# Values of 64-feature heads as the stationary operand, in two column tiles

## The reference, cut to what matters

```
s = q @ k.T * scale + bias[distance]          # causal
p = exp(s - max(s));  den = sum(p)            # rows of p are queries
y = (p @ v) / den                             # v: keys x 64 features
mix = concat(y of 8 heads of 64, y of 4 heads of 128) @ w_out
```

## Time and profile before

| | us |
|---|---|
| median of 3 runs | 2202.65 (2201.94 to 4978.07) |
| the profiled execution, its own time | 2203.65 |
| its span, first to last instruction | 2201.7 |
| MOBA units 8 to 15 | about 1156 to 1213 in the span |
| dil units 16 to 23 | about 1696 to 1755 in the span |

### The profile page before, as it was taken

The page is one execution under the profiler, slowest core; times in us unless marked ns, Lnnn a source line. Parts: engine busy times, 40 slices in busy tenths (PEclk is TensorE's granted clock), DMA queues, the critical chain, the costliest instruction groups (busy, mean ns, idle before and its releaser), DMA issues.

```text
span 2201.7 us, 27538 instructions
## 1 busy us (share of the span) xinstructions
PE 2173.0 (99%) x10078; PEld 1790.0 (81%) x10078; DVE 844.8 (38%) x1310; ACT 845.1 (38%) x1193; POOL 1048.5 (48%) x883
## 2 busy tenths in 40 slices
PE   8999999999999999999999999999999999999998
PEld 6778778888888888888888888888887888888887
DVE  4244666632451111222366633331226645232212
ACT  4245665422242222222366433332324734333321
POOL 5431244655544444555454354445554534444553
PEclk9999999999999999999999999999999999999999
DMA  5222122332223222333221232222332212222232
GB/s 180 88 78 77 39 88 85 99 111 96 96 85 107 95 95 78 105 104 99 103 63 63 77 115 95 95 77 93 108 113 91 74 47 96 95 95 98 84 103 78
DMA packets 33992, 201.89 MB, mean 92 GB/s; under 512 B 3900, under 2 KB 6204, under 8 KB 15484
## 3 DMA queue, kind: packets, MB, share of 16 engines
q1 hardware_dynamic: 31532, 192.94, 25.7%
q0 software_dynamic: 2384, 7.92, 1.1%
HBM read 198.69 MB, written 2.15 MB: 91 GB/s over the span
## 4 chain that ended last, share of the span: by engine, by line
PE 94%; DVE 3%; issue 1%; POOL 1%; ACT 1%; DMA 0%; DVEq 0%; SPq 0%; POOLq 0%; PEldq 0%; ACTq 0%
PE bank L417 28%; PE bank L419 28%; PE bank L418 28%; PE bank L660 2%; PE bank L958 1%; PE bank L647 1%; PE bank L918 1%; PE bank L972 1%; DVE pool_a L2346 1%; DVE temp_b L2162 0%; PE bank L634 0%; PE bank L633 0%; PE bank L630 0%; PE bank L1018 0%; PE bank L1019 0%
## 5 line engine op out<-in xcount | busy, mean ns | idle before, releaser
L1145 POOL TENSOR_TENSOR w_low<-raw,w_high 128x512 fp32r<-128x512 f32 (+2 forms) x768 | 961.3, 1283 | 1042.5 <-ACT w_high L1309 1004.1
L417 PE MATMUL bank<-x_low,w_high 128*128 128x512 f32 x1728 | 680.6, 394 | 13.1 <-DVE x_low L2158 9.4
L419 PE MATMUL bank<-x_high,w_low 128*128 128x512 f32 x1728 | 673.3, 390 | 0.0
L418 PE MATMUL bank<-x_high,w_high 128*128 128x512 f32 x1728 | 673.0, 389 | 0.0
L1309 ACT ACTIVATE w_high<-raw 128x2048 fp32r<-128x2048 f32 (+1 forms) x183 | 327.5, 1789 | 538.3 <-PE bank L419 538.3
L417 PEld LDWEIGHTS bank<-x_low,w_high 128*128 128x128 f32 x1728 | 324.8, 188 | 85.0 <-POOL w_low L1228 9.4
L418 PEld LDWEIGHTS bank<-x_high,w_high 128*128 128x128 f32 x1728 | 324.9, 188 | 68.5 <-issue 2.2
L419 PEld LDWEIGHTS bank<-x_high,w_low 128*128 128x128 f32 x1728 | 324.6, 188 | 68.3
L417 PE MATMUL bank<-act_low,w_high 128*128 128x512 f32 (+1 forms) x550 | 209.4, 381 | 0.0
L418 PE MATMUL bank<-act_high,w_high 128*128 128x512 f32 (+1 forms) x550 | 209.3, 381 | 0.0
L419 PE MATMUL bank<-act_high,w_low 128*128 128x512 f32 (+1 forms) x550 | 209.3, 380 | 0.0
(11 more groups left out here) (292 smaller groups left out, 2700.4 us busy)
## 6 DMA issues: line engine op xcount, KB each, us to landing
raw<-wmain SPq DMA_DIRECT2D x144, 1024.0 KB, 4.9
raw<-wdown SPq DMA_DIRECT2D x48, 704.0 KB, 4.0
bias<-distance_table POOLq DMA_DIRECT2D x24, 256.0 KB, 3.5
raw<-wmain SPq DMA_DIRECT2D x4, 512.0 KB, 8.5
x_residual<-x SPq DMA_DIRECT2D x4, 512.0 KB, 7.4
out<-qk SPq DMA_DIRECT2D x8, 256.0 KB, 2.2
matrices<-mats SPq DMA_DIRECT2D x1, 512.0 KB, 11.2
r_blocks<-rg POOLq DMA_DIRECT2D x1, 512.0 KB, 6.6
```

Of the source, the lines that this page charges most:

```text
L417: pe.matmul(target, sh, ml, start=start and k == 0, stop=False)
L418: pe.matmul(target, sh, mh, start=False, stop=False)
L419: last = pe.matmul(target, sl, mh, start=False, stop=stop and k == n - 1)
L1145: pool.tensor_tensor(wl[:, c, part], raw[:, c, part], wh[:, c, part].bitcast(F32), ALU.subtract).then_inc(low_ready, 1)
```

## The change

For MOBA and dil pairs, nothing is multiplied with the values in the even unit. Its turned probabilities are kept in `yt` (which no longer holds these heads' results). In the odd unit, `values` takes both heads: for each key block two matmuls, one for each head, with the 64 values of the head as the stationary operand and 128 turned probabilities as the moving one. The even unit's head takes column tile 0 and writes partitions 0 to 63 of bank 6, the odd one's takes column tile 64 and writes partitions 64 to 127. The result has features on the partitions and needs no turn. The norm factors, which are one for each token, are spread by DVE over 64 columns for each head (`rd` to `gs`), turned by PE with four transposes into a spare bank (`factors`), copied to `gs` by DVE, and multiplied with bank 6 back into the spare bank (`pair_normalised`); from there ACT and DVE take the high and low parts as before. The MOBA pairs' factors are turned in fills of units 10, 12 and 14 and in `project_out`. Renaming a helper (`paired` to `two_inputs`) changes nothing.

```diff
+def result_at(g):
+    return g // 2 if g < MLA else MLA // 2 + g - MLA
+
+def paired(g):
+    return MOBA <= g < MLA
+
-             + [("eturn", 2), ("eturn", 3)] + [("eout", t) for t in range(6)]
+             + [("eturn", 2), ("eturn", 3), ("eout", 0), ("eturn", 4), ("eout", 1), ("eout", 2), ("eturn", 5), ("eout", 3)]
+             + [("eout", 4), ("eturn", 6), ("eout", 5), ("eturn", 7)]
...
+        def turned(g, b):
+            if paired(g) and g % 2 == 0:
+                return yt[:, b, 0:(b + 1) * P]
+            return pts[:, b % 2, 0:(b + 1) * P]
...
             def values(g, b):
                 kind, m, u = UNITS[g]
+                if paired(g) and u == 0:
+                    return
                 v = turn_at(g)
                 pe.wait_ge(sem("pt_odd" if b % 2 else "pt_even"), 2 * v + b // 2 + 1)
-                if b == 0 and v:
-                    pe.wait_ge(sem("y_read"), v)
...
+                if b == 0 and result_at(g):
+                    pe.wait_ge(sem("y_read"), result_at(g))
+                if paired(g):
+                    for k in range(b + 1):
+                        for j, turned in enumerate((yt, pts)):
+                            at = 64 * j
+                            last = pe.matmul(bank[6][at:at + 64, b * P:(b + 1) * P], vt[:, k, m * P + at:m * P + at + 64],
+                                             turned[:, b % (2 if j else NB), k * P:(k + 1) * P], start=k == 0, stop=k == b,
+                                             tile_position=(0, at))
+                    last.then_inc(sem("pv_done"), 1)
+                    return
...
+            def factors(target, n):
+                pe.wait_ge(sem("rd_ready"), n + 1)
+                for b in range(NB):
+                    last = pe.transpose(target[:, b * P:(b + 1) * P], gs[:, n // HEADS, b * P:(b + 1) * P], ident)
+                return last
...
             def token_turn(n):
-                target = spare(("oturn", n))
-                pe.wait_ge(sem("y_read"), turn_at(DIL + 2 * n + 2))
-                turn(target, n).then_inc(sem("spare_ready"), 1)
+                factors(spare(("oturn", n)), HEADS + n).then_inc(sem("spare_ready"), 1)
...
                 elif g < DIL:
                     at = 4 * (g - 9) + b - 3
+                    if g % 2 == 0 and b == 3:
+                        factors(spare(("eturn", g // 2 - 1)), g // 2 - 5).then_inc(sem("spare_ready"), 1)
                     if at < 24:
                         first_half("eout", at // 4, at % 4)
...
-                    pe.wait_ge(sem("y_read"), turn_at(units) - heads * (3 - h))
-                    turn(bank[TURN_BANK[h]], first + h).then_inc(sem("turned"), 1)
+                    if name == "oout":
+                        pe.wait_ge(sem("y_read"), result_at(units) - (3 - h))
+                        turn(bank[TURN_BANK[h]], first + h).then_inc(sem("turned"), 1)
+                    elif h == 3:
+                        factors(spare(("eturn", 7)), 3).then_inc(sem("spare_ready"), 1)
...
+                        if t == 0 and name == "eout":
+                            spare_free(pe, ("eturn", HEADS + k))
...
             def normalised(g):
                 kind, n, u = UNITS[g]
-                dve.wait_ge(sem("pv_done"), 4 * turn_at(g) + 4)
+                if paired(g):
+                    dve.wait_ge(sem("p_ready"), score_at(g, 3) + 1)
+                    step(dve.reciprocal(rd[:, u, :], rs[:, u, :]))
+                    if u:
...
+                        dve.tensor_copy(gs[:, int(g > DIL), :].rearrange("p (b u f) -> p b u f", b=NB, u=2),
+                                        rd.rearrange("p u b -> p b u").unsqueeze(3).to_broadcast([P, NB, 2, 64]))\
+                           .then_inc(sem("rd_ready"), 1)
+                    return
...
+            def pair_normalised(r, target):
+                spread = gs[:, r // HEADS - 1, :]
+                step(dve.tensor_copy(spread, target))
+                dve.wait_ge(sem("pv_done"), 4 * r + 4)
+                dve.tensor_tensor(target, bank[6][:, :], spread, ALU.mult).then_inc(sem("y_read"), 1)
...
                     if b == 2:
                         half_added("eout", g - 10)
+                    if g % 2 == 0 and b == 3:
+                        dve.wait_ge(sem("spare_ready"), SPARE["eturn", g // 2 - 1] + 1)
+                        pair_normalised(g // 2 - 1, spare_bank(("eturn", g // 2 - 1)))
+                    if g % 2 and b == 0 and g > 10:
+                        pair_turn(g // 2 - 5)
```

More of the change, by code:

```diff
@@ L512, in token_major, with two_inputs @@
                                 behind_first()
[L514 removed]
+            def two_inputs(name, chunks, x0, x1, ready, read0, read1, free_after, x0_ready=None, x1_ready=None,
                        norm=None, at=0, free=None):
@@ L827, in fill, with project_out @@
                         first_half("oout", n // 4, n % 4)
-            def project_out(name, ready, read, units, turned):
-                first, heads = YT[name, 1], 2 if name == "eout" else 1
+            def project_out(name, ready, read, units):
+                first = YT[name, 1]
                 pe.wait_ge(sem("s_read"), 4 * units)
@@ L1425, in copy_even @@
                 if n >= 2:
-                    act.wait_ge(sem("pv_done"), n - 1)
-                act.activation(pts[:, 0, 0:(b + 1) * P], bank[4][:, 0:(b + 1) * P], ACT.Copy)\
-                   .then_inc(sem("pt_even"), 1)
+                    act.wait_ge(sem("pv_done"), copy_after(g, b))
+                act.activation(turned(g, b), bank[4][:, 0:(b + 1) * P], ACT.Copy).then_inc(sem("pt_even"), 1)
             def spare_refill(use, c, n, second):
@@ L1550, in spare_out @@
                     head_turn(2 + b // 2)
+                elif MOBA < g < DIL and g % 2 == 0 and b == 3:
+                    pair_turn(g // 2 - 5)
                 elif (g, b) == (MLA, 0):
@@ L1563, in spare_out, with project_out @@
                         mla_copy(("uv", n), vt[:, n, S:2 * S])
-            def project_out(name, ready, read, v, gain, g0, turned):
-                for h in range(4):
-                    act.wait_ge(sem("turned"), turned + h + 1)
-                    turn_high(name, 1, h, bank[TURN_BANK[h]][:, :])
+            def project_out(name, ready, read, v, gain, g0):
+                if name == "eout":
+                    pair_turn(3)
+                else:
+                    for h in range(4):
+                        act.wait_ge(sem("turned"), h + 1)
+                        turn_high(name, 1, h, bank[TURN_BANK[h]][:, :])
                 refill(1, BASE[name] + 3)
@@ L1989, in copy_odd @@
                 if n >= 2:
-                    dve.wait_ge(sem("pv_done"), n - 1)
-                dve.tensor_copy(pts[:, 1, 0:(b + 1) * P], bank[5][:, 0:(b + 1) * P]).then_inc(sem("pt_odd"), 1)
+                    dve.wait_ge(sem("pv_done"), copy_after(g, b))
+                dve.tensor_copy(turned(g, b), bank[5][:, 0:(b + 1) * P]).then_inc(sem("pt_odd"), 1)
             def blocks(t, n=P):
@@ L2147, in project_out @@
             def project_out(name, ready, read, v, gain, g0, high):
-                for h in range(4):
-                    turn_low(name, 1, h, bank[TURN_BANK[h]][:, :], high + h + 1, sem("turn_read"))
+                if name == "eout":
+                    dve.wait_ge(sem("spare_ready"), SPARE["eturn", 7] + 1)
+                    pair_normalised(result_at(DIL) - 1, spare_bank(("eturn", 7)))
+                    pair_turn(3)
+                else:
+                    for h in range(4):
+                        turn_low(name, 1, h, bank[TURN_BANK[h]][:, :], high + h + 1, sem("turn_read"))
                 spare_free(dve, (name, 4), (name, 5))
```

45 lines of the change are left out of this document (31 added, 14 removed).

## The result

The changed kernel takes **2206.97 us** (median of 18 runs, 2204.36 to 2209.84), the kernel before 2202.77 beside it: ratio 1.0019, 95% interval 1.0013 to 1.0026. So it is 4.2 us slower, where 5.6 us faster was forecast. The profiled execution of after took 2209.16 us, near the top of its runs, that of before 2203.65; what is read from the two traces therefore adds up to 5.5 us. One run of the kernel before took 4978.07 us and stands outside the ratio.

What follows compares the result with a forecast made beforehand. PE, busy for 99% of the span, was taken as the bound. Values and switches -7.5, dil's turns -0.7, projection's end +1.1 and new waits +1.5 gave -5.6 us: a median of 2197 us, range 2190 to 2206.

Steps and rivals of the forecast that it cites:

- Values and switches: MOBA and dil pairs: side-by-side tiles plus three switches of 0.34 take 3.22 us instead of 4.16; 7.5 us gained in all.
- two rivals: Tiled value blocks: weight loads not hidden, about 2206 us (5%); tiles take turns, about 2214 us (7%).
- The projection's end: Projection behind MOBA: the last operand waits for DVE's copy and multiplication of the turned factors, +1.1 us (0.7 to 1.4).
- The new waits: Paired stretches: DVE's and ACT's added factor work is mostly hidden, +1.5 us, between -1 and +9.7.
- The sign that the prediction named: Forecast is wrong if PE's idle time before the values (L681) or transposes (L665) grows by more than 3 us.
- The clock: Rival: more idle time on PE in dil could bring four clock drops, +6.8 us, near 2204; 3%.
- the waits take it back: Rival: DVE and ACT fall behind at seven places, +9.7 instead of +1.5, about 2205 us; 15%.
- the 15% rival: DVE and ACT fall behind at seven places in the paired stretches, +9.7 instead of +1.5, about 2205 us; 15%.
- The new order of the spare banks: Paired stretches: spare banks come free about as far ahead of the next fill's need as before; cost nothing.
- +1.5 - 0.7: Paired stretches: +1.5 us of new waits for DVE and ACT, -0.7 as dil's turns stop waiting for the factors' product.
- the 9.7 less 0.7 of the rival: +9.7 us if DVE and ACT fall behind at seven places (15%), less 0.7 of dil's turns' waits that go.

Runs made afterwards that it cites:

- e5: Changed kernel with the values of step 0 taken in step 2, so two tiled blocks for a pair instead of three: 2205.95 us.
- e3: Changed kernel with ACT making both high parts of the next stack in step 0 of the unit: 2202.89 us.
- e4: Kernel before with ACT making both high parts of the next stack in step 0 of the unit: 2201.9 us.
- e13: Changed kernel with POOL's swap copies cut to 128 of 512 columns for units 10 to 15 and 18 to 23: 2204.05 us.
- e14: Kernel before with POOL's swap copies cut to 128 of 512 columns for units 10 to 15 and 18 to 23: 2203.04 us.
- e15: Changed kernel with 18 unread fp32 products in three of PE's waits (ahead of first scores of units 10, 18 and MLA): 2205.55 us.
- e6: Changed kernel with MOBA's fills dealt as six quarters to an even unit and two to an odd one, not four and four: 2216.48 us.
- e8: Changed kernel with all of tile 0's value matmuls ahead of all of tile 64's in each step: 2209.37 us.
- e11: Changed kernel with early stack high parts and two tiled blocks for a pair, but only MOBA's heads paired in tiles: 2202.69 us.

## Why the prediction was wrong, by its steps

**Values and switches: right.** 8.8 us gained by the blocks of the trace, 7.5 forecast. The switch is 0.28 (e5) where 0.34 was taken from the stage with four tiles. The loads are hidden and the tiles don't take turns: two rivals fell. The Trainium skill, "TensorE: Matmul & The Clock Gate", Part 3, has loads overlap "only when row_grp differs", though the same part also lets them run ahead into a background weight buffer; the trace disagrees with the first as a rule for column tiles, with both tiles' loads of 0.14 us under passes that start every 0.11.

**The projection's end: right.** 0.93 us of wait, 1.1 forecast.

**The new waits: this is the step that failed.** It said +1.5, with DVE and ACT as what limits, and looked at DVE's and ACT's sums and at the one chain that the change adds. It never asked what else is due once in a unit. Taking 2.08 us out of every even unit and putting 1.0 into the odd one shortens a deadline: the stack chain, 6.2 us (7.6 the first time) from the unit's start, now has 5.65. 2.6 us of it are POOL's. It costs 2.0 us in unit 9, 0.6 in units 11 and 13, and 3.4 in dil. By e3 beside e4 and e13 beside e14 it makes up 3.2 of the 4.2 us by which the change is slower, clock drops included. That is about a third of the 9.8 us between the forecast's -5.6 and the measured +4.2; the rest is in large part waits for ACT and DVE, below, which are located but not told apart. The sign that the prediction named, 3 us more idle time ahead of the values and the transposes, looked past it: there it is 3.3 us, against 3.0 before. It stands ahead of the scores (L651), 6.4 us against 0.5. The rows to see it by were in the trace of before: a slack of 1.1 us in a steady unit, and the 0.23 that PE waited at 1163.41.

**The clock** was priced as a rival by itself, with 3%. Here it doesn't come by itself: both drops stand behind waits of PE and are missing where these are filled (e15), so it belongs to the case "the waits take it back". The drops of the profiled execution cost 3.1 us, the one of the kernel before 1.3 (unit 18, 9.14 us against 7.82 in e4); e15 puts the medians' share at 1.4 to 2.4.

**The rest** is the mechanism of the 15% rival, at places it didn't name: unit 15, where no scores cover ACT's copy (1.4 us), and dil, where spare banks and copies are late. The new order of the spare banks was put at nothing there; PE waits 1.7 us in dil for DVE's low part (L2159), which frees a bank, and 0.9 and 1.0 for copies of turned probabilities. e6 shows the queue on ACT that it described, with the cover gone: 2.4 us at a place.

**The range** ended at 2206 because each rival was added to the forecast alone. The sum by the profiled pair: -8.8 for the values, +0.9 for the projection, waits from 1.2 to 4.1 in MOBA and unit 15 and from 3.2 to 9.2 in dil (+8.9, where +1.5 - 0.7 stood), and +1.8 for the clock: +2.8. The spans differ by 5.5, of which 1.1 stand ahead of unit 8 and behind unit 27, where the kernels are alike. So 1.6 us of the loss are in no row of the waits; 0.5 of it is the part of the late scores in units 11 and 13 that the modelled ends hide (0.59 each, 0.35 in the view), and the rest stays open. That the waits' +8.9 comes so near to the 9.7 less 0.7 of the rival is luck: they stand at other places.

## What to carry to other kernels

When work leaves one unit of a software pipeline for another, list every chain that must end once in each unit, on whatever engine, with its length from the unit's start, and compare it with the new length of the shortest unit; busy shares say nothing about it (POOL stood at 47%). An average gain over two units is worth less where a chain that can't begin before its own unit sets the length of the shorter one. And price a stall with the clock drop that may follow it, in one case and not in two.

## What the runs showed of the hardware

- Two column tiles fed turn and turn about start their passes within 0.01 us and every 0.11 us, with 64-column loads of 0.14 hidden. Fed one after the other, they still ran side by side except for two passes at the start, two in the middle and four at the end (e8, 2.17 us for 28 passes instead of 1.68). The Trainium skill, "TensorE: Matmul & The Clock Gate", Part 3, says that matmuls start strictly in program order; in e8's rows a pass of tile 64 starts at 1200.29, ahead of one of tile 0 that the program lists before it and that starts at 1200.39.
- After 2.0 us of idle PE the granted clock went to 0.50 some 1.5 us later and stayed there for 3.4 us. With 1.95 us of unread products in the same wait it didn't (e15). The drop of 3.4 us cost 1.2 (unit 9, 10.72 us against 9.55).
- The same kernel can have more such drops in one execution than in another: the changed kernel's runs have mean clocks from 0.999 (2204.36 us) to 0.995 (2209.84). Between e4 and e11 one drop is worth 1.5 us in unit 18, where both have the same instructions.
